# The causal mask of the differential attention: added on VectorE in PSUM, or accumulated by identity products on TensorE

## The chip, the cores and the metric

The kernel runs on one core of one Trainium2 chip. The metric is the time of one execution on the device in microseconds, as the median of several runs.

## What is computed

A decoder trunk of two layers over 512 tokens of width 1024, in fp32. Layer 0 mixes tokens with an mLSTM, layer 1 with a causal differential softmax attention; both also attend to 256 memory tokens, and both end with a gated feed-forward block. The part of the change is the differential attention, cut here to what matters:

```python
def diff_attention(h, positions, w_in, q_norm, k_norm, lam_vecs, subln, lambda_init):
    p = h @ w_in
    q = rope(rmsnorm(p[..., :768].reshape(B, S, 12, 64), q_norm), positions)
    k = rope(rmsnorm(p[..., 768:1536].reshape(B, S, 12, 64), k_norm), positions)
    v = p[..., 1536:2304].reshape(B, S, 6, 128)
    def block(qblk, bi):                                   # 128 query rows
        s = einsum('bhqd,bhkd->bhqk', qblk, kh) * scale
        s = where(key_idx[None, :] <= q_idx[:, None], s, -inf)      # the causal mask
        pr = softmax(s, axis=-1).reshape(B, 6, 2, 128, S)
        a = pr[:, :, 0] - lam * pr[:, :, 1]
        return einsum('bhqk,bhke->bhqe', a, vh)
```

## The kernel before

The program is written by hand for each engine: one instruction stream per engine, and semaphores between them. The order of the work is the order of the statements in each stream; no planner moves it.

*Dense tiles.* Every projection is a row of tiles of 128 output columns. A tile (`h_tile`, `a_tile`, through `tile`, lines 1265 to 1282) runs over eight blocks k of 128 input rows, and for each it issues three products with a moving side of 512 columns (high weight by high input, high by low, low by high), so 24 in all. All of them, and every other plain product, go through the helper `mm` and show as line 1248. GpSimd splits each weight tile into w_hi and w_lo (lines 461 and 464); it starts a split when TensorE has finished the tile two before (`dense_done`). VectorE takes a finished tile out of PSUM and scales it (`scaled_out`, line 907).

*The differential attention.* It runs over six heads, c = 0 to 5, each of two half heads of 64 rows. Its steps are threaded between the products of the next head's three dense tiles q, k and v: `in_q`, `in_k` and `in_v` are called after the three products of block k of a tile. Per head, TensorE issues four score blocks `b_s(c, u)`, u = 0 to 3, which belong to the query rows t = 3 - u and have (t + 1) x 128 columns: 512, 384, 256 and 128. Block u writes the banks b and b + 1 with b = 6 - 2 (u % 2), so blocks 0 and 2 share banks 6 and 7, and blocks 1 and 3 share 4 and 5. In the k tile stand block 0 (after k = 4) and block 1 (after k = 7, the tile's end), in the v tile block 2 (after k = 0) and block 3 (after k = 2). Blocks 2 and 3 wait until ScalarE has finished the exponentials of the block two before (`bexp`, line 1590). The last head has no dense tile behind it: blocks 2 and 3, the transposes and two small sums stand in a row (lines 1655 to 1664).

For each block, VectorE (`b_max`, lines 1177 to 1185) waits for `bs_done`, adds the mask to the diagonal 128 columns in PSUM (line 1182), takes the maximum of each row (line 1184) and scales it (line 1185, a product of 128x2 elements). `link` is a helper that makes VectorE wait for its own last instruction. ScalarE takes the exponentials (`b_exp`, line 745), VectorE forms the difference of the two probabilities (`b_prob`, lines 1194 to 1196), TensorE transposes it (`b_t`, line 1604), ScalarE copies it out as ATB (line 754), and `b_pv` (line 1611, shown as line 1248) multiplies it with the values, VB. `b_ss` sums the squares of q and k with a selector of 2 columns, half_sel (shown as line 1248, from QS). VectorE's order in a head is block 0's maximum, the k tile taken out, then `b_max` 1, `b_prob` 0, `b_max` 2, `b_prob` 1, `b_max` 3, `b_prob` 2 and 3 (lines 1218 to 1226).

`ident` and `neg_mask` are 128x128 fp32 constants in SBUF, parts of the tile `cn`: the identity, and -1e30 above the diagonal with 0 elsewhere.

Of the kernel before, what the change touches and what calls it, by code (L numbers as in the profile page):

```python
# [28 lines left out]
ALU = mybir.AluOpType  # L29
# [3 lines left out]
P = 128  # L33
# [87 lines left out]
def hybrid_trunk(nc, x, mem, positions, w_out, w_mem_kv, w_gate_up, w_down, a_w_in, a_gate_b, b_w_in,  # L121
                 b_lambda, prm_rows, con, out):
    ctx = ExitStack()
    with ctx:
        def sb(name, shape, dt=F32, scope=ctx):
            return scope.enter_context(nc.sbuf_tensor(name, shape, dt))
# [4 lines left out]
        PS = ctx.enter_context(nc.psum_tensor("PS", [P, 8, 512], F32))  # L131
# [24 lines left out]
        ident = cn[:, C_ID:C_ID + P]  # L156
# [3 lines left out]
        neg_mask = cn[:, C_NEG:C_NEG + P]  # L160
# [43 lines left out]
        QR = sb("QR", [P, 2, SEQ], scope=sB)  # L204
# [616 lines left out]
        def _(dve):  # L821
            link_n = [0]

            def link(ins):
                link_n[0] += 1
                ins.then_inc(vch, 1)
                dve.wait_ge(vch, link_n[0])
# [349 lines left out]
            def b_max(c, u):  # L1177
                t, b = NT - 1 - u, 6 - 2 * (u % 2)
                n = 4 * c + u
                dve.wait_ge(bs_done, n + 1)  # L1180
                dg = PS[:, b:b + 2, t * P:(t + 1) * P]
                link(nc.vector.tensor_tensor(dg, dg, neg_mask.rearrange("p (a n) -> p a n", a=1).broadcast_to([P, 2, P]), ALU.add))
                j = (8 * c + 2 * u) % 64
                link(nc.vector.tensor_reduce(nmB[:, j:j + 2], PS[:, b:b + 2, 0:(t + 1) * P], AX.X, ALU.max, negate=True))  # L1184
                nc.vector.tensor_tensor(nmB[:, j:j + 2], nmB[:, j:j + 2], rqk_all[:, 0, t], ALU.mult).then_inc(bmax, 1)  # L1185
# [19 lines left out]
            for c in range(MC):  # L1205
                n = T_B + 3 * (c + 1)
                last = c + 1 == MC
                if c == 0:
                    dve.wait_ge(trig, 2)
                b_rope(c)  # L1210
                b_norm(c)
                if c >= 1:
                    b_onorm(c - 1)
                scaled_out(n, xqB[:, 0] if last else QKP[:, (c + 1) % 2, 0])
                b_knorm(c)
                if c >= 1:
                    b_lo(c - 1)
                b_max(c, 0)
                scaled_out(n + 1, xqB[:, 1] if last else QKP[:, (c + 1) % 2, 1])
                b_max(c, 1)  # L1220
                b_prob(c, 0)
                b_max(c, 2)
                b_prob(c, 1)
                b_max(c, 3)
                b_prob(c, 2)
                b_prob(c, 3)
                if not last:
                    if c >= 1:
                        dve.wait_ge(bvt_done, c)
                    scaled_out(n + 2, t512[2 + (c + 1) % 2])  # L1230
# [15 lines left out]
        def _(pe):  # L1246
            def mm(out_, a, b, start=True, stop=True):
                return nc.tensor.matmul(out_, a, b, start=start, stop=stop)  # L1248
# [50 lines left out]
            for k in range(KD):  # L1299
                pe.wait_ge(msq_done, k // 2 + 1)  # L1300
                last = mm(PS[:, 3, 0:MEM], ones[:], msq[:, k], start=k == 0, stop=k == KD - 1)
# [52 lines left out]
            for i, row in enumerate((tmp[6], tmp[0])):  # L1354
                for t in range(NT):
                    last = nc.tensor.transpose(PS[:, 3, (i * NT + t) * MH:(i * NT + t + 1) * MH], row[0:MH, t * P:(t + 1) * P],
                                               ident[0:MH, 0:MH])
# [225 lines left out]
            def b_s(c, u):  # L1583
                t, b = NT - 1 - u, 6 - 2 * (u % 2)
                if u == 0:
                    pe.wait_ge(bkr, c + 1)
                if u == 1 and c >= 1:
                    pe.wait_ge(bmix_lo, c)
                if u >= 2:
                    pe.wait_ge(bexp, 2 * (4 * c + u - 2) + 2)  # L1590
                for hd in range(2):
                    r = 64 * hd
                    last = mm(PS[:, b + hd, 0:(t + 1) * P], QR[r:r + 64, 0, t * P:(t + 1) * P], QR[r:r + 64, 1, 0:(t + 1) * P])
                last.then_inc(bs_done, 1)

            def b_t(c, u):
# [17 lines left out]
            for c in range(MC):  # L1614
                n = T_B + 3 * (c + 1)
# [11 lines left out]
                def in_k(k):  # L1627

                    if k < 2:
                        b_kbc(c, 2 * k)  # L1630
                        b_kbc(c, 2 * k + 1)
                    if c >= 1 and k in (2, 3):
                        b_oturn(c - 1, 2 * (k - 2))
                        b_oturn(c - 1, 2 * (k - 2) + 1)
                    if k == 4:
                        b_s(c, 0)
                    if k in (5, 6):
                        b_vt(c, 2 * (k - 5))
                        b_vt(c, 2 * (k - 5) + 1)
                    if k == 7:  # L1640
                        b_s(c, 1)

                def in_v(k):

                    if k in (0, 2):
                        b_s(c, 2 + k // 2)
                    if k in (5, 6):
                        b_t(c, k - 5)
# [72 lines left out]
```

## Time and profile before

| | us |
|---|---|
| median of 3 runs | 1361.65 |
| lowest and highest run | 1358.72, 1362.04 |
| span of the profiled execution | 1360.3 |
| TensorE busy (products) | 1288.3 |
| TensorE busy (weight loads) | 1029.4 |
| VectorE busy | 654.4 |
| GpSimd busy | 724.3 |
| ScalarE busy | 344.8 |

A timeline row gives start and duration in us, with equal neighbours merged ("x4"), and in brackets the idle time before it and what ended it. A group row ends with the idle time before its instructions and who ended that. Lines are those of the kernel before.

### The profile page before, as it was taken

To read this page: it belongs to the slowest core of one execution; us is meant where nothing else is said; L and a number is where in the kernel's file an instruction comes from. 1 tells how busy PE (TensorE), PEld (TensorE's weight loads), DVE (VectorE), ACT (ScalarE), POOL (GpSimd) and SP (SyncE) were. 2 spreads that over 40 slices of the span, in tenths; PEclk is the share of its full clock that TensorE was granted. 3 is DMA by queue.
4 is the path that set the end of the run, shared out by engine and by line. 5 is a ranking of instruction groups with operands and counts; after the bars stand their busy time and mean duration, and the time that the engine had idled before them with its cause. 6 is when DMAs were issued, how large, how long until landed. Compare 5 with 4: busy or idle time off the path is not lost.

```text
span 1360.3 us, 16185 instructions
## 1 busy us (share of the span) xinstructions
PE 1288.3 (95%) x5865; PEld 1029.4 (76%) x5865; DVE 654.4 (48%) x804; ACT 344.8 (25%) x679; POOL 724.3 (53%) x422
## 2 busy tenths in 40 slices
PE   5789999988999999999999799988999999999998
PEld 5667767666888888888887577666888888888886
DVE  6788812365734213322368777773753313331331
ACT  5332312355222001100122444456232100100101
POOL 5555543223666666666666333430666666666663
PEclk9898989998999999999999899998999999999999
DMA  8322221111333333333233222220333333333322
GB/s 246 83 62 77 79 77 31 47 47 31 94 97 103 93 93 94 106 94 93 87 106 111 65 73 78 64 76 0 93 93 94 93 96 105 93 93 95 102 74 86
DMA packets 217840, 116.34 MB, mean 86 GB/s; under 512 B 3912, under 2 KB 216002, under 8 KB 217794
## 3 DMA queue, kind: packets, MB, share of 16 engines
q1 hardware_dynamic: 216208, 111.69, 28.4%
q10 hardware_dynamic: 1586, 4.07, 1.1%
q8 instruction: 26, 0.43, 0.1%
q14 instruction: 20, 0.16, 0.0%
HBM read 110.50 MB, written 2.10 MB: 83 GB/s over the span
## 4 chain that ended last, share of the span: by engine, by line
PE 78%; DVE 14%; ACT 3%; issue 2%; POOL 1%; DMA 1%; ACTq 0%; DVEq 0%; POOLq 0%
PE PS L1248 76%; DVE QK L927 2%; DVE acc L870 2%; DVE Al L847 1%; DVE QK L924 1%; POOL w_lo L464 1%; DVE nmB L1185 1%; DVE tmp L917 1%; POOL w_hi L461 1%; DVE nmB L1184 1%; DMA prm<-in_rows_dram 1%; DVE kvs L898 0%; DVE xT L1083 0%; PE PS L1604 0%; DVE Al L1021 0%
## 5 line engine op out<-in xcount | busy, mean ns | idle before, releaser
L461 POOL TENSOR_SCALAR w_hi<-w_raw 128x1024 fp32r<-128x1024 f32 (+1 forms) x207 | 218.7, 1057 | 606.2 <-PE PS L1248 597.5
L464 POOL TENSOR_TENSOR w_lo<-w_raw,w_hi 128x1024 fp32r<-128x1024 f32 (+1 forms) x207 | 505.3, 2441 | 17.3
L1248 PE MATMUL PS<-Hh,w_hi 128*128 128x512 f32 x1080 | 437.5, 405 | 17.2 <-issue 8.1
L1248 PE MATMUL PS<-Hh,w_lo 128*128 128x512 f32 x1080 | 423.6, 392 | 0.0
L1248 PE MATMUL PS<-Hl,w_hi 128*128 128x512 f32 x1080 | 423.5, 392 | 0.0
L1248 PEld LDWEIGHTS PS<-Hh,w_hi 128*128 128x128 f32 x1080 | 204.8, 190 | 72.3 <-issue 22.1
L1248 PEld LDWEIGHTS PS<-Hh,w_lo 128*128 128x128 f32 x1080 | 204.3, 189 | 43.9
L1248 PEld LDWEIGHTS PS<-Hl,w_hi 128*128 128x128 f32 x1080 | 205.0, 190 | 38.3 <-issue 0.7
L1248 PE MATMUL PS<-Ah,w_hi 128*128 128x512 f32 (+1 forms) x544 | 209.8, 386 | 8.8 <-DVE kv L856 4.4
L1248 PE MATMUL PS<-Ah,w_lo 128*128 128x512 f32 (+1 forms) x544 | 205.9, 379 | 0.0
L1248 PE MATMUL PS<-Al,w_hi 128*128 128x512 f32 (+1 forms) x544 | 205.9, 378 | 0.0
L1248 PEld LDWEIGHTS PS<-Ah,w_hi 128*128 128x128 f32 x544 | 103.3, 190 | 33.9 <-issue 4.6
L1099 DVE TENSOR_TENSOR tmp<-PS,rinv 128x512 f32<-128x512 f32 x44 | 30.4, 692 | 200.4 <-PE PS L1248 200.4
L1248 PEld LDWEIGHTS PS<-Ah,w_lo 128*128 128x128 f32 x544 | 103.3, 190 | 19.0
L1248 PEld LDWEIGHTS PS<-Al,w_hi 128*128 128x128 f32 x544 | 103.4, 190 | 17.5
L691 ACT ACTIVATE tmp<-tmp 128x512 f32<-128x512 f32 x44 | 27.9, 634 | 317.7 <-DVE tmp L1097 317.7
L1105 DVE TENSOR_TENSOR Al<-tmp,Ah 128x512 f32 x44 | 82.3, 1871 | 40.1 <-ACT Ah L693 40.1
L693 ACT ACTIVATE Ah<-tmp 128x512 f32 x44 | 27.9, 633 | 251.6 <-DVE tmp L1102 251.6
L1114 DVE TENSOR_TENSOR xT<-xT,PS 128x512 f32 x32 | 22.0, 688 | 137.9 <-PE PS L1248 137.9
L870 DVE TENSOR_TENSOR acc<-acc,tmp 128x512 f32<-128x512 f32 x28 | 67.5, 2411 | 14.7 <-ACT tmp L518 14.7
L1097 DVE TENSOR_TENSOR tmp<-PS,rinv 128x512 f32<-128x512 f32 x44 | 30.4, 692 | 53.8 <-PE PS L1248 53.4
L518 ACT ACTIVATE tmp<-xT 128x512 f32<-128x512 f32 x32 | 20.3, 635 | 101.9 <-DVE xT L1083 91.8
(249 smaller groups left out, 1077.3 us busy)
## 6 DMA issues: line engine op xcount, KB each, us to landing
w_raw<-in_w_gate_up_dram SPq DMA_DIRECT2D x88, 512.0 KB, 3.8
w_raw<-in_w_down_dram SPq DMA_DIRECT2D x32, 512.0 KB, 3.6
w_raw<-in_a_w_in_dram SPq DMA_DIRECT2D x27, 512.0 KB, 3.8
w_raw<-in_b_w_in_dram SPq DMA_DIRECT2D x20, 512.0 KB, 3.8
w_raw<-in_w_out_dram SPq DMA_DIRECT2D x16, 512.0 KB, 3.6
w_raw<-in_w_down_dram SPq DMA_DIRECT2D x16, 384.0 KB, 3.1
w_raw<-in_w_mem_kv_dram SPq DMA_DIRECT2D x8, 512.0 KB, 7.9
QKR<-QKP ACTq DMA_DIRECT2D x24, 128.0 KB, 4.8
```

Of the source, the lines that this page charges most:

```text
L461: nc.gpsimd.tensor_scalar(w_hi[:, sl, 0:nk], w_raw[:, raw, 0:nk], 0.0, 1.0, ALU.add, ALU.mult).then_inc(w_round, 1)
L464: nc.gpsimd.tensor_tensor(w_lo[:, sl, 0:nk], w_raw[:, raw, 0:nk], w_hi[:, sl, 0:nk].bitcast(F32), ALU.subtract).then_inc(w_split, 1)
L518: nc.scalar.activation(tmp[6 + n % 2][:, 0:SEQ], xT[:, k], ACT.Square).then_inc(xsq, 1)
L691: nc.scalar.activation(tmp[0][:, 0:SEQ], tmp[1][:, 0:SEQ], ACT.Silu).then_inc(silu_done, 1)
L693: nc.scalar.activation(Ah[:, bass.ds(i, 1)], tmp[3][:, 0:SEQ].rearrange("p (a n) -> p a n", a=1), ACT.Copy).then_inc(f_hi, 1)
L870: nc.vector.tensor_tensor(acc[:], acc[:], sq, ALU.add).then_inc(xsq_used, 1)
L927: nc.vector.scalar_tensor_tensor(y, raw[:, tap:tap + SEQ], w(R_CW + tap * QKC), y, ALU.mult, ALU.add).then_inc(conv_step if tap else conv_ ...
L1097: nc.vector.tensor_tensor(tmp[1][:, 0:SEQ], PS[:, base % 2], rinv[:], ALU.mult).then_inc(dense_free, 1)
L1099: nc.vector.tensor_tensor(tmp[2][:, 0:SEQ], PS[:, (base + 1) % 2], rinv[:], ALU.mult).then_inc(dense_free, 1)
L1105: nc.vector.tensor_tensor(Al[:, bass.ds(i, 1)], one, Ah[:, bass.ds(i, 1)].bitcast(F32), ALU.subtract).then_inc(f_ready, 1)
L1114: nc.vector.tensor_tensor(xk_, xk_, PS[:, b:b + 1], ALU.add).then_inc(dense_free, 1)
L1248: return nc.tensor.matmul(out_, a, b, start=start, stop=stop)
```

## The change

VectorE no longer adds the mask. In its place TensorE, behind the two score products of a block, issues two more products, one for each half head, with the identity as stationary and the mask as moving side, which accumulate onto the diagonal 128 columns of the scores in PSUM. `bs_done` is raised by the last of these.

```diff
@@ b_max, VectorE @@
                 dve.wait_ge(bs_done, n + 1)
-                dg = PS[:, b:b + 2, t * P:(t + 1) * P]
-                link(nc.vector.tensor_tensor(dg, dg, neg_mask.rearrange("p (a n) -> p a n", a=1).broadcast_to([P, 2, P]), ALU.add))
                 j = (8 * c + 2 * u) % 64
@@ b_s, TensorE @@
                 for hd in range(2):
                     r = 64 * hd
-                    last = mm(PS[:, b + hd, 0:(t + 1) * P], QR[r:r + 64, 0, t * P:(t + 1) * P], QR[r:r + 64, 1, 0:(t + 1) * P])
+                    mm(PS[:, b + hd, 0:(t + 1) * P], QR[r:r + 64, 0, t * P:(t + 1) * P], QR[r:r + 64, 1, 0:(t + 1) * P],
+                       stop=False)
+                for hd in range(2):
+                    last = mm(PS[:, b + hd, t * P:(t + 1) * P], ident, neg_mask, start=False)
                 last.then_inc(bs_done, 1)
```

## Rows read from the trace of the kernel before

**Rows 1.** The page: TensorE's busy time and share, and the ended-last chain by engine.
```profile
PE 1288.3 (95%) x5865; PEld 1029.4 (76%) x5865; DVE 654.4 (48%) x804; ACT 344.8 (25%) x679; POOL 724.3 (53%) x422
...
PE 78%; DVE 14%; ACT 3%; issue 2%; POOL 1%; DMA 1%; ACTq 0%; DVEq 0%; POOLq 0%
```

**Rows 2.** Busy times in a stretch of head 2: length, PE, PEld, DVE, ACT, POOL, clock, DMA.
```profile
815.00:843.00 28.00, 26.75 (x147) 20.32 (x146) 22.12 (x39) 13.18 (x35) 10.18 (x7) 1.00 0.27 76
```

**Rows 3.** TensorE's waits, 759 to 918 us: waiting line, releaser, us in total, times, longest.
```profile
PE PS L1248 <- ACT PB L745: 8.8, 6, 2.6
```

**Rows 4.** Timeline, TensorE, head 2: start us, us, engine, line, op, tiles, shape, count [idle].
```profile
822.54 0.92 PE L1248 MATMUL PS<-QR 64*128 64x384 f32 x4
823.38 0.50 PE L1248 MATMUL PS<-Hh,w_hi 128*128 128x512 f32 x1
...
824.28 0.70 PE L1248 MATMUL PS<-QR 64*128 64x256 f32 x4
...
825.94 0.39 PE L1248 MATMUL PS<-Hl,w_hi 128*128 128x512 f32 x1
826.17 0.40 PE L1248 MATMUL PS<-Hh,w_lo 128*128 128x512 f32 x1
827.82 0.49 PE L1248 MATMUL PS<-QR 64*128 64x128 f32 x4 [1.25 <-ACT PB L745]
828.25 0.50 PE L1248 MATMUL PS<-Hh,w_hi 128*128 128x512 f32 x1
```

**Rows 5.** Timeline, TensorE, head 2: fp32 products of 128 rows, narrow and wide.
```profile
835.90 0.50 PE L1248 MATMUL PS<-cn,QS 128*128 128x2 f32 x4
836.26 0.48 PE L1248 MATMUL PS<-Hh,w_hi 128*128 128x512 f32 x1
...
837.41 2.48 PE L1248 MATMUL PS<-VB,ATB 128*128 128x128 f32 x20
839.64 0.47 PE L1248 MATMUL PS<-Hh,w_hi 128*128 128x512 f32 x1
```

**Rows 6.** Groups by line and form, 759 to 918 us: the mask addition (count | busy us, mean ns).
```profile
L1182 DVE TENSOR_TENSOR PS<-PS,cn 128x256 f32<-128x256 f32 x24 | 10.3, 429 | 5.9 <-PE PS L1248 5.9
```

**Rows 7.** Timeline, VectorE, head 2, around the second score block.
```profile
823.50 0.43 DVE L1182 TENSOR_TENSOR PS<-PS,cn 128x256 f32<-128x256 f32 x1 [0.16 <-PE PS L1248]
823.97 0.96 DVE L1184 TENSOR_REDUCE nmB<-PS 128x2 f32<-128x768 f32 x1
824.96 1.36 DVE L1185 TENSOR_TENSOR nmB<-nmB,rqk_all 128x2 f32<-128x2 f32 x1
```

**Rows 8.** Line L1185 of VectorE: shortest, median and longest of its 24 instructions, in ns.
```profile
L1185 DVE TENSOR_TENSOR nmB<-nmB,rqk_all x24: 160/161/1360, 765.4 to 915.5; 128x2 f32<-128x2 f32 x24
```

**Rows 9.** Timeline, GpSimd, heads 1 and 2: the weight split that runs beside block 1.
```profile
795.77 2.38 POOL L464 TENSOR_TENSOR w_lo<-w_raw,w_hi 128x1024 fp32r<-128x1024 f32 x1
...
822.77 1.06 POOL L461 TENSOR_SCALAR w_hi<-w_raw 128x1024 fp32r<-128x1024 f32 x1 [4.60 <-PE PS L1248]
823.91 2.39 POOL L464 TENSOR_TENSOR w_lo<-w_raw,w_hi 128x1024 fp32r<-128x1024 f32 x1
```

**Rows 10.** Timeline, TensorE, last head, from its fourth score block on.
```profile
912.17 0.80 PE L1248 MATMUL PS<-QR 64*128 64x128 f32 x4 [2.62 <-ACT PB L745]
...
914.67 0.90 PE L1604 MATMUL PS<-cn,PB 128*128 128x128 f32 x3 [0.66 <-DVE PB L1196]
...
917.27 0.88 PE L1604 MATMUL PS<-cn,PB 128*128 128x128 f32 x3 [0.20 <-ACT ATB L754]
918.57 4.13 PE L1248 MATMUL PS<-VB,ATB 128*128 128x128 f32 x20 [0.43 <-ACT ATB L754]
922.63 1.99 PE L1248 MATMUL PS<-xk,xqB 64*128 64x256 f32 x8
```

**Rows 11.** Stretches of 1 us in the last head: clock in the column before the DMA share.
```profile
910.00:911.00 1.00, 0.00 (x0) 0.00 (x0) 0.96 (x3) 0.30 (x1) 0.65 (x1) 1.00 0.00 0
...
912.00:913.00 1.00, 0.83 (x5) 0.61 (x6) 0.96 (x3) 0.63 (x3) 0.00 (x0) 0.50 0.85 254
```

## The prediction

> **What bounds the kernel now.** I read the page first. TensorE is busy for 1288.3 us and holds 78% of the chain that ended last; VectorE holds 14% [rows 1]. That is an average over stages, so I went to the stage of the change, the differential attention from 759 to 918 us: six heads (c = 0 to 5), each with four score blocks (u = 0 to 3, of 512, 384, 256 and 128 columns). In the stretch of head 2, TensorE is busy for 26.75 of 28 us at the full clock, and VectorE for 22.12 [rows 2]. One head takes 28.1 us: the same step of GpSimd starts at 795.77 and 823.91 [rows 9]. The list of TensorE's waits says where the rest is: six waits on the exponentials of line 745, 8.8 us together, which is one per head, 1.25 us in a steady head and 2.6 in the last [rows 3, 4, 10]. So in heads 0 to 4 TensorE sets the pace with one stall per head, and work that is added to TensorE costs its full time unless it falls into that stall. VectorE's saving counts only through the stall.
>
> Where the stall lies decides the sum. The timeline of TensorE shows the order: block 1 starts at 822.54, block 2 at 824.28, the last weight product before the stall at 826.17, then nothing until block 3 at 827.82 [rows 4]. Weight products follow each other every 0.23 us (825.94, 826.17). Behind block 1 the three products from 823.38 to block 2 take 0.90 us and not 0.69: 0.11 is a weight load that isn't hidden behind a score block, 0.10 the change to the next one. So block 3 could have started at 826.17 + 0.23 + 0.10 = 826.50, and the spare time is 1.32 us. Block 3 waits for the exponentials of block 1, since both use banks 4 and 5. These follow line 1185 of block 1, which ends at 824.96 + 1.36 = 826.32 [rows 7]. Line 1185 is a product of 128x2 elements. Its median is 161 ns and here it takes 1360 [rows 8]. GpSimd's subtraction of a weight tile runs from 823.91 to 826.30 [rows 9], and line 1185 ends 0.02 us after it; both read two SBUF tensors. The end of the stall is therefore pinned by GpSimd, whose split was released by the end of the k tile, ahead of block 1, and not by VectorE's own length.
>
> **The change part by part.** *Removed:* 24 additions on VectorE, 429 ns each, 10.3 us in all [rows 6], and one link wait each: from the addition's start to that of the reduction are 0.47 us [rows 7]. *Added:* two fp32 products per block on TensorE, 48 in all, stationary the identity of 128x128, moving the 128x128 mask. The semaphore bs_done moves to the last of them. No DMA, buffer or instruction of ScalarE or GpSimd is added or moved.
>
> The price of a mask product. The nearest row is the product of weights and values: same type, same 128x128 stationary, same 128 columns. Ten of them leave 20 records, and the next product starts 2.23 us later (837.41 to 839.64) [rows 5], or 0.112 us a record and 0.223 a product. Two fp32 products with only 2 moving columns take 0.36 us until the next product starts [rows 5], nearly the 0.45 of a pair with 128 columns. The price hangs on the weight load, not on the columns. A block of two mask products costs 0.446 us. The load of 0.11 us that is exposed behind a score block today is exposed once after the change too, so it cancels. From below the bound is the column time: from a score block to the next product are 0.43 us with 128 columns (827.82 to 828.25) and 0.84 with 384 (822.54 to 823.38) [rows 4], so 128 columns more cost four records 0.205 us, and the four of a mask block would cost 0.21. A block could cost less than that only by running beside other products, and TensorE's records follow each other in order, which excludes a gain here. From above: 0.89, if each product took twice the records seen. I take 0.446, of the row with the same shape.
>
> *Block 0 (heads 0 to 5).* TensorE goes on with the k tile after it and waits for nothing. The two products are exposed: +0.446 us. On VectorE the result comes 0.446 later and the addition's 0.47 is gone, so its maximum is ready at the same moment; ScalarE and all behind it stay.
>
> *Blocks 1 and 2 (heads 0 to 4).* Both are issued between the k tile and the stall. Block 1's scores come 0.446 later, the reduction starts at 823.94 in place of 823.97, and line 1185 is held until 826.30 as before. The stall ends at the same distance from the k tile; 0.89 us of mask work comes ahead of it and takes 0.89 of the 1.32 us of spare time. Cost: 0, and the cover is not used up (0.43 left). Were it gone, up to 0.89 a head would come on top. Queued behind TensorE's wait for block 3 is the rest of the v tile, the same as now.
>
> *Block 3 (heads 0 to 4).* It starts when the stall ends and nothing waits behind it: +0.446 us. VectorE saves two additions after the stall, 0.9 us, so the transposes of the weights, which TensorE reaches 0.45 later, find them ready. What is late next is nothing that I can see; TensorE is the bound until the next head's stall. The dense tiles that follow shift with it.
>
> *Head 5.* It has no v tile, and TensorE waits four times: 2.62, 0.66, 0.20 and 0.43 us [rows 10]. Block 0 costs 0.446. Blocks 1 and 2 vanish in the 2.62. Block 3 runs at the half clock [rows 11]. There 20 records take 4.06 us (918.57 to 922.63) [rows 10], so it costs 0.81, against 0.66 of wait behind it. That wait is for VectorE, which is one addition ahead there, and two ahead at the waits of 0.20 and 0.43. I take back 0.3 more than block 3 costs (bounds 0 and 0.7). Head 5: +0.45 - 0.3 = +0.15.
>
> *The sum.* 5 heads x 2 exposed blocks x 0.446 = 4.46, and 0.15: +4.6 us. The profiled execution has a span of 1360.3 us, which becomes 1364.9. The runs' median is 1361.65, 1.35 above that span, so 1366.2 us on the runs. That is 0.34% more, and 0.3% (4.1 us, 1365.7) is about what a measurement of this kernel can tell from no change. The runs of before themselves lie 3.3 us apart.
>
> The Trainium skill would price a record lower: its page "TensorE: Matmul & The Clock Gate" (Back-to-back issue gap) gives about 81 ns for a pair of weight load and product with 128 columns. By it a block would be 0.32 us, and the ten exposed ones 3.2 us. The trace has 112 ns for this shape and type, and the sum goes by the trace.
>
> **The rivals.**
>
> *The clock stays up in the last head (not slower).* TensorE falls to half its clock, from 2.4 to 1.2 GHz, between 911 and 913 us after standing still [rows 11]. With the masks of blocks 1 and 2 the engine stands still for 1.7 us and not 2.6. If the clock then holds, the weights-and-values product takes 2.23 us in place of 4.06, and the waits ahead of it shrink by some 0.8 to 1.2. That is -2.6 us on head 5: 4.6 - 2.6 = +2.0, or 1363.7 us. It decides if the clock's fall is later than 919 us in the new trace. Against it: several waits remain between short products in 912 to 918. 0.14.
>
> *A mask product costs only its columns.* Same stationary twice, small moving tile: 0.21 a block gives 10 x 0.21 + 0.1 = 2.2, or 1363.9 us. Against it: products with 2 columns cost nearly as much as those with 128 [rows 5]. 0.08.
>
> *The stall does not cover.* If line 1185 is not pinned by GpSimd but follows from when its inputs are ready and then always takes 1.36 us, the end of the stall still stays (+0.446 - 0.47). Only if the hold starts anew behind the mask does it move: the stall then ends 0.45 to 0.9 later, all four blocks count, 20 x 0.446 = 8.9 and 0.5 for head 5, or 1371 us. Against it: 826.30 and 826.32 agree to 0.02 us [rows 7, 9]. 0.10.
>
> *An fp32 product takes four passes.* Then a block costs 0.89, two are 1.78 in a spare time of 1.32, and a head pays 2 x 0.89 + 0.46 = 2.24; five heads 11.2 and about 1 in the last: 1374 us. In the trace the same product has two records of 0.112 us each, so I give it 0.03. The Trainium skill states this rule: "FP8 and Floating Point Precision" (TensorE Precision Notes) has true fp32 at four passes through the array. By that rule the sum would be the one of this rival; the trace disagrees with it.
>
> *Faster.* By over 0.3% would need 8.7 us below the forecast. The half clock would have to go in both later dips, and I find no row that promises it. 0.03.
>
> **How the numbers follow.** Forecast 0.62, clock 0.14, columns only 0.08, no cover 0.10, four passes 0.03, faster 0.03 (sum 1.00). The forecast's own spread is about 1 us around 1366.2, with the border at 1365.7, so two thirds of it (0.42) is slower and 0.20 the same. Slower: 0.42 + 0.10 + 0.03 = 0.55. Same: 0.20 + 0.14 + 0.08 = 0.42. Faster: 0.03. The range takes in the clock case with its spread below and the case without cover above: 1362 to 1371 us. What is outside is the four passes, the faster case and some tails.
>
> **What the new profile would show.** Right: after each score block in heads 0 to 4, four more records of TensorE, 128x128 by 128 columns, with 0.44 to 0.45 us until the next product; the period of a head at 29.0 us; TensorE's wait before block 3 at about 0.4 us; line 1185 of block 1 (now two lines higher) still ending with GpSimd's subtraction; VectorE's busy time in the stage lower by 10.3 us. Wrong: a period near 28.5 (cheap products), near 29.9 (no cover) or above 30 (four passes); a clock in the last head that does not fall (first rival). If the period is 29.0 and the time still differs by more than 2 us, the difference lies in the dips of the clock behind 910 us.

## The result and the profile after

| | before | after |
|---|---|---|
| median of 17 runs, us | 1360.73 | 1364.46 |
| lowest and highest run, us | 1356.55, 1363.22 | 1361.56, 1367.37 |
| span of the profiled execution, us | 1360.3 | 1364.3 |

The ratio of the runs is 1.0031, with a 95% interval from 1.0020 to 1.0042: slower by 0.31%, or 4.2 us, where 4.6 was forecast (the two medians alone differ by 3.7). The profiled spans differ by 4.0 us.

The page of the changed kernel, its busy times:

```profile
PE 1297.1 (95%) x5961; PEld 1038.3 (76%) x5961; DVE 643.3 (47%) x780; ACT 344.8 (25%) x679; POOL 725.7 (53%) x422
```

TensorE is busy 8.8 us longer and VectorE 11.1 us shorter than in [rows 1], and the time follows neither. A stretch of 28 us in head 2 (length; busy time and count of PE, PEld, DVE, ACT and POOL; clock, DMA share, GB/s), and the waits of TensorE from 759 to 923 us (waiting line, releaser, us in total, times, longest):

```profile
820.00:848.00 28.00, 27.68 (x158) 21.39 (x157) 20.14 (x34) 13.17 (x35) 9.56 (x7) 1.00 0.27 76
```

```profile
PE PS L1246 <- ACT PB L745: 3.2, 6, 1.6
```

TensorE is busy 27.68 us of 28, where [rows 2] have 26.75. Its six waits on the exponentials shrink from 8.8 us [rows 3] to 3.2. The timeline of TensorE in head 2 shows where the added products went (start us, us, engine, line, op, tiles, shape, count, idle before):

```profile
825.19 0.92 PE L1246 MATMUL PS<-QR 64*128 64x384 f32 x4
826.04 0.71 PE L1246 MATMUL PS<-cn 128*128 128x128 f32 x4
826.50 0.48 PE L1246 MATMUL PS<-Hh,w_hi 128*128 128x512 f32 x1
...
827.38 0.70 PE L1246 MATMUL PS<-QR 64*128 64x256 f32 x4
828.01 0.71 PE L1246 MATMUL PS<-cn 128*128 128x128 f32 x4
...
830.43 0.49 PE L1246 MATMUL PS<-QR 64*128 64x128 f32 x4 [0.32 <-ACT PB L745]
830.86 0.71 PE L1246 MATMUL PS<-cn 128*128 128x128 f32 x4
831.32 0.48 PE L1246 MATMUL PS<-Hh,w_hi 128*128 128x512 f32 x1
```

Each mask block is four records named `PS<-cn`. Two numbers carry the case. Block 1's mask starts at 826.04 and the next weight product at 826.50, so a block takes 0.46 to 0.47 us here. The net is slightly less: from block 1 to block 2 are 2.19 us (825.19 to 827.38), where they were 1.74 [rows 4], so the mask adds 0.45, and the head period below gives 0.44. And the wait before block 3 is 0.32 us, where it was 1.25 [rows 4]. VectorE's reduction and the small product of block 1, and GpSimd's subtraction beside them:

```profile
826.79 0.96 DVE L1182 TENSOR_REDUCE nmB<-PS 128x2 f32<-128x768 f32 x1 [0.80 <-PE PS L1246]
827.78 1.15 DVE L1183 TENSOR_TENSOR nmB<-nmB,rqk_all 128x2 f32<-128x2 f32 x1
```

```profile
826.55 2.36 POOL L464 TENSOR_TENSOR w_lo<-w_raw,w_hi 128x1024 fp32r<-128x1024 f32 x1
```

The small product (now line 1183) ends at 828.93, GpSimd's subtraction at 828.91: the same 0.02 us as in [rows 7, 9]. VectorE now idles 0.80 us before the reduction, where it idled 0.16 before the addition. Of the 0.64 us more, 0.47 are the addition that it no longer does. The other 0.17 are new: the reduction starts 1.60 us after block 1's first product (825.19), and the addition started 0.96 after it (822.54, 823.50), so the mask makes the scores 0.64 us late and not only the 0.45 that it costs TensorE. GpSimd's hold covers this too.

### The profile page after: what moved, and what is told of

Same layout as the page of the kernel before. It is cut to its first block, busy times and chain, and to the rows that moved or that the text cites. A ratio compares the mean times of both kernels' runs of the same rounds, so it can differ in the third digit from the quotient of the medians.

```text
span 1364.3 us, 16353 instructions
## 1 busy us (share of the span) xinstructions
PE 1297.1 (95%) x5961; PEld 1038.3 (76%) x5961; DVE 643.3 (47%) x780; ACT 344.8 (25%) x679; POOL 725.7 (53%) x422
## 4 chain that ended last, share of the span: by engine, by line
PE 78%; DVE 13%; ACT 3%; issue 2%; POOL 1%; DMA 1%; ACTq 0%; DVEq 0%; POOLq 0%
PE PS L1246 76%; DVE QK L927 2%; DVE acc L870 2%; DVE Al L847 1%; DVE QK L924 1%; POOL w_lo L464 1%; DVE tmp L917 1%; DVE nmB L1183 1%; POOL w_hi L461 1%; DMA prm<-in_rows_dram 1%; PE PS L1605 1%; DVE kvs L898 0%; DVE nmB L1182 0%; DVE xT L1083 0%; DVE Al L1021 0%
```

## Where the 4.0 us of the profiled pair are

The first two rows below are of the kernel before: block 0 of head 0, and block 0 of the last head; the third is the first product of the output projection behind the attention.

```profile
762.51 1.13 PE L1248 MATMUL PS<-QR 64*128 64x512 f32 x4
...
903.16 1.13 PE L1248 MATMUL PS<-QR 64*128 64x512 f32 x4
...
946.10 0.50 PE L1248 MATMUL PS<-Ah,w_hi 128*128 128x512 f32 x1
```

The kernel after: block 0 of head 0, then from block 0 of the last head to the same product of the output projection:

```profile
762.94 1.13 PE L1246 MATMUL PS<-QR 64*128 64x512 f32 x4
...
907.96 1.13 PE L1246 MATMUL PS<-QR 64*128 64x512 f32 x4
...
917.41 0.49 PE L1246 MATMUL PS<-QR 64*128 64x128 f32 x4 [1.60 <-ACT PB L745]
...
919.45 0.90 PE L1605 MATMUL PS<-cn,PB 128*128 128x128 f32 x3 [0.47 <-DVE PB L1194]
...
921.71 0.88 PE L1605 MATMUL PS<-cn,PB 128*128 128x128 f32 x3
923.02 3.86 PE L1246 MATMUL PS<-VB,ATB 128*128 128x128 f32 x20 [0.43 <-ACT ATB L754]
926.81 1.99 PE L1246 MATMUL PS<-xk,xqB 64*128 64x256 f32 x8
...
950.17 0.50 PE L1246 MATMUL PS<-Ah,w_hi 128*128 128x512 f32 x1
```

Block 0 of head 0 starts 0.43 us later than before: that lies ahead of everything the change touches. From there to the last head's block 0 are 145.02 us and not 140.65: +4.37 for five heads, 0.87 each (forecast 0.89). From that block to the output projection are 42.21 us and not 42.94: -0.73 (forecast +0.15). The rest of the program gives 0.07 back. 0.43 + 4.37 - 0.73 - 0.07 = 4.0.

The 0.73 us can be followed through the rows. Up to the second batch of transposes nothing changes: it starts 11.51 us after block 0 before (914.67 and 903.16) and 11.49 after (919.45 and 907.96). In both kernels TensorE waits for VectorE there, and the one addition of 0.47 us that VectorE has saved by then pays for block 0's mask. From there to the third batch are 2.26 us and not 2.60: the wait for ScalarE's copy (0.20 us [rows 10]) is gone, because VectorE is a second addition ahead and the copy starts 0.48 us earlier in the head (12.89 us after block 0, 13.37 before). The product of weights and values takes 3.79 us (923.02 to 926.81) in place of 4.06 [rows 10], and all that follows up to the output projection 0.11 less.

The clock moved as well. Two stretches of 1 us of the kernel after (the clock is the column after the five engines):

```profile
918.00:919.00 1.00, 0.98 (x8) 0.75 (x8) 0.93 (x4) 0.82 (x3) 0.00 (x0) 1.00 1.07 322
919.00:920.00 1.00, 0.55 (x3) 0.55 (x4) 0.96 (x4) 0.42 (x3) 0.00 (x0) 0.54 0.02 4
```

TensorE falls from 2.4 to 1.2 GHz at about 919 us; before, it was at 0.50 from 912 on [rows 11]. With the shift of 4.8 us taken off, that is some 2.5 us later, so block 3 of the last head, its mask and the first transposes run at the full clock. But a late fall is not the only way to such a gain. In the run with blocks 0 and 3 on TensorE (below), the clock had fallen ahead of block 3 (granted 0.50 from 916 to 917 us), and the last head, from block 0 to the output projection, still takes 42.30 us:

```profile
907.55 1.13 PE L1249 MATMUL PS<-QR 64*128 64x512 f32 x4
...
917.00 0.80 PE L1249 MATMUL PS<-QR 64*128 64x128 f32 x4 [2.62 <-ACT PB L745]
917.73 1.22 PE L1249 MATMUL PS<-cn 128*128 128x128 f32 x4
...
949.85 0.50 PE L1249 MATMUL PS<-Ah,w_hi 128*128 128x512 f32 x1
```

Block 3's mask takes 1.02 us there until the next product, at half the clock, and the waits of 0.66 and 0.20 us behind it are gone. Up to the product of weights and values (923.12) the last head takes 15.57 us in that run, 15.41 before and 15.06 after. The rest of its gain lies in that product, 3.52 us, during which the clock rises. So of the 0.73 us up to 0.5 can be the late fall, and no run separates it from VectorE's lead. One profile of each does not tell how much repeats: the product of weights and values of the last head takes between 3.5 and 4.6 us over the profiles of this case.

## The experiments

In all of them the head period is the distance between block 0 of one head and of the next. It repeats to 0.05 us within a profile unless said otherwise, and it is the sharpest measure here; the ratios have an interval of 0.1 to 0.2% to each side. It is 28.13 us before and 29.00 after.

**Only blocks 1 and 2 on TensorE.**

```diff
 b_max:
+                if u in (0, 3):
                     dg = PS[:, b:b + 2, t * P:(t + 1) * P]
                     link(nc.vector.tensor_tensor(dg, dg, neg_mask..., ALU.add))
 b_s:
+                if u in (1, 2):
+                    for hd in range(2):
+                        last = mm(PS[:, b + hd, t * P:(t + 1) * P], ident, neg_mask, start=False)
```

> Kernel before, but the masks of score blocks 1 and 2 go to TensorE; blocks 0 and 3 keep VectorE's addition. Theory (the stall ahead of block 3 covers blocks 1 and 2): the head period stays at 28.13 us as in the kernel before, TensorE's wait before block 3 is 0.3 to 0.4 us, the last head gains 0 to 0.5 us, and the time is that of before within 0.1% (ratio 0.999 to 1.001). Rival (every mask block costs TensorE its 0.44 us wherever it stands, the wait only moves): period 29.0 us, ratio about 1.003. Rival (cost shared evenly over four blocks): period 28.57 us, ratio 1.0015.

Ratio 1.0006 (0.9996 to 1.0017), period 28.11 us. Blocks 0, 3 and the next 0 in TensorE's timeline:

```profile
786.26 1.13 PE L1249 MATMUL PS<-QR 64*128 64x512 f32 x4
...
795.29 0.49 PE L1249 MATMUL PS<-QR 64*128 64x128 f32 x4 [0.32 <-ACT PB L745]
...
814.36 1.13 PE L1249 MATMUL PS<-QR 64*128 64x512 f32 x4
```

The two blocks are in the program, the period is that of before, and the wait before block 3 fell from 1.25 to 0.32 us. Mask work in the stall costs nothing. The last head gained 0.66 us (42.28 against 42.94), a little more than the 0 to 0.5 expected.

**Only blocks 0 and 3 on TensorE.** The same edit with the blocks exchanged.

> Kernel before, but the masks of score blocks 0 and 3 go to TensorE; blocks 1 and 2 keep VectorE's addition. Theory (only blocks 0 and 3 are exposed): head period 29.0 us, that of the changed kernel, with TensorE's wait before block 3 at 1.25 us as before; about +4.4 us over the five heads, ratio 1.003 to 1.004. Rival (shared evenly): period 28.57, ratio 1.0015.

Ratio 1.0023 (1.0012 to 1.0034), period 29.02 us:

```profile
791.48 1.13 PE L1249 MATMUL PS<-QR 64*128 64x512 f32 x4
...
800.98 0.49 PE L1249 MATMUL PS<-QR 64*128 64x128 f32 x4 [1.23 <-ACT PB L745]
...
820.51 1.13 PE L1249 MATMUL PS<-QR 64*128 64x512 f32 x4
```

The full loss per head with half of the added products, and the wait is still 1.23 us. The ratio is below the 1.003 to 1.004 expected, though its interval reaches into that; the 0.64 us that the last head gains (42.30 against 42.94) are part of the reason. So the loss of the change is that of blocks 0 and 3. The even split of the cost is out.

**No mask at all.** Both lines of the addition in `b_max` are deleted from the kernel before, and nothing is put in their place.

> The causal mask is left out altogether, on both engines (this part of the computation is missing). Theory (the end of the stall is pinned by GpSimd's subtraction): head period 28.13 us as before, though VectorE is 0.47 us shorter per block; the product of 128x2 elements in block 1 then takes about 1.8 us and still ends with GpSimd's subtraction; only the last head gains, 0.3 to 0.9 us; ratio 0.9993 to 1.0. Rival (VectorE's own length sets the end of the stall): the stall shrinks by 0.47 us, period 27.66 us, -2.4 us and the last head on top, ratio 0.998.

Ratio 0.9992 (0.9982 to 1.0002), period 28.13 us. VectorE's reduction and small product of block 1, and GpSimd's subtraction:

```profile
794.70 0.96 DVE L1182 TENSOR_REDUCE nmB<-PS 128x2 f32<-128x768 f32 x1 [0.16 <-PE PS L1246]
795.69 1.81 DVE L1183 TENSOR_TENSOR nmB<-nmB,rqk_all 128x2 f32<-128x2 f32 x1
```

```profile
795.10 2.38 POOL L464 TENSOR_TENSOR w_lo<-w_raw,w_hi 128x1024 fp32r<-128x1024 f32 x1
```

Without the addition VectorE starts both steps 0.46 us earlier in the head, the small product takes 1.81 us in place of 1.36, and it still ends with GpSimd's subtraction (797.50 and 797.48). VectorE's 10.3 us of additions in [rows 6] cost the kernel before nothing in heads 0 to 4. In these heads there was nothing for the change to win. The last head gained 0.71 us (42.23 against 42.94).

**The small product in another form, in all blocks.** In the kernel before, line 1185 becomes two instructions that read one SBUF tensor and a scalar of one column each:

```diff
-                nc.vector.tensor_tensor(nmB[:, j:j + 2], nmB[:, j:j + 2], rqk_all[:, 0, t], ALU.mult).then_inc(bmax, 1)
+                for hd in range(2):
+                    ins = nc.vector.tensor_scalar(nmB[:, j + hd:j + hd + 1], nmB[:, j + hd:j + hd + 1],
+                                                  rqk_all[:, 0, t, hd:hd + 1], None, ALU.mult)
+                ins.then_inc(bmax, 1)
```

> Kernel before with VectorE's addition kept in all blocks; only the product of 128x2 elements that reads two SBUF tensors is written as two tensor_scalar instructions of 128x1, each with one SBUF tensor and one scalar of a column. Theory (that product is held because it reads two SBUF tensors while GpSimd's subtraction runs): in block 1 it takes 0.2 to 0.35 us in place of 1.36, the stall ahead of block 3 shrinks by about 1.0 us to 0.2, the head period falls to 27.1 to 27.3 us unless a later wait appears before the last transposes, and the time falls by 4 to 5 us (ratio 0.9965 to 0.997). Rival (the 1.36 us have another cause, such as the write or the position behind the reduction): period 28.1 to 28.5 us, ratio 1.000 to 1.001.

Ratio 1.0147 (1.0125 to 1.0169): slower by 20 us (18 between the medians), where 4 to 5 us faster was expected. TensorE's waits, then VectorE (block 1's split product, and the last two steps of the same head), then GpSimd:

```profile
PE PS L1607 <- DVE PB L1199: 6.9, 5, 1.4
PE PS L1251 <- ACT PB L745: 1.2, 5, 0.2
```

```profile
831.42 0.33 DVE L1186 TENSOR_SCALAR nmB<-nmB,rqk_all 128x1 f32<-128x1 f32 x2
...
838.92 0.76 DVE L1198 TENSOR_SCALAR PB<-PB,rsB,lam 128x128 f32<-128x128 f32 x1
839.71 2.48 DVE L1199 SCALAR_TENSOR_TENSOR PB<-PB,rsB 128x128 f32<-128x128 f32 x1
```

```profile
838.33 1.27 POOL L461 TENSOR_SCALAR w_hi<-w_raw 128x1024 fp32r<-128x1024 f32 x1 [5.59 <-PE PS L1251]
839.68 2.36 POOL L464 TENSOR_TENSOR w_lo<-w_raw,w_hi 128x1024 fp32r<-128x1024 f32 x1
```

Half of the expectation came true. The split product takes 0.33 us in place of 1.36 while GpSimd subtracts (830.36 to 832.74), and the waits before block 3 in heads 0 to 4 fell from 1.23 to 1.25 us each to 0.23. This agrees with the rule of the Trainium skill's page "SBUF — State Buffer" (Who interferes with whom): a VectorE instruction with two SBUF inputs contends with a GpSimd instruction that reads SBUF, one with at most one such input, outside the 2-port modes, does not. The form with one SBUF tensor is not free of the hold by itself, though: VectorE's next step, a tensor_scalar of 128x512, takes 1.16 us in this run (from 831.86, over the end of GpSimd's subtraction) and 0.55 in the changed kernel (829.04), where the subtraction has ended. No trace shows in which mode it runs.

What I had not worked out is the end of the head. TensorE arrives about 1 us earlier at the end of the v tile, so GpSimd begins its next split earlier too, but VectorE has hardly become faster: line 1198 starts 13.70 us after block 0 (838.92), and 13.77 before. Its last two steps (lines 1198 and 1199 of this kernel) now meet it: the first runs until 839.68, when w_hi is done, and the second starts at 839.71, just behind GpSimd's subtraction of 839.68, and takes 2.48 us for 128x128 elements. TensorE waits up to 1.4 us for it before the last transpose, then its clock falls in four of the five heads (granted 0.90 to 0.94 over a head, 1.00 over head 0), and the period goes to 29.4, 32.6, 30.9, 31.0 and 32.6 us.

**The same in block 1 alone.**

```diff
+                if u == 1:
+                    (the two tensor_scalar as above)
+                else:
                     nc.vector.tensor_tensor(nmB[:, j:j + 2], nmB[:, j:j + 2], rqk_all[:, 0, t], ALU.mult).then_inc(bmax, 1)
```

> Kernel before with all four additions on VectorE; only block 1's product of 128x2 elements is split. Theory (the split gains at the stall and loses at the end of the head, because VectorE with its four additions begins its last combination behind GpSimd's next subtraction): TensorE waits about 0.2 us before block 3 and over 1 us for line 1196 before the last transpose, the clock falls in some heads, head period above 29 us, ratio 1.005 to 1.015. Rival (the late hold in the run with all products split came from the 0.17 us that each further split costs): no late wait, period 27.0 to 27.1 us, ratio about 0.996.

Ratio 1.0079 (1.0058 to 1.0100), periods 29.14, 32.38, 29.13, 32.35 and 29.17 us. GpSimd, then VectorE's last two steps of head 1:

```profile
804.87 1.04 POOL L461 TENSOR_SCALAR w_hi<-w_raw 128x1024 fp32r<-128x1024 f32 x1 [5.60 <-PE PS L1254]
```

```profile
805.10 0.89 DVE L1201 TENSOR_SCALAR PB<-PB,rsB,lam 128x128 f32<-128x128 f32 x1
806.03 2.48 DVE L1202 SCALAR_TENSOR_TENSOR PB<-PB,rsB 128x128 f32<-128x128 f32 x1
```

The last combination takes 2.47 to 2.48 us in heads 0 to 4, and TensorE waits for it once in each, 7.5 us in all. The extra instructions of the other blocks were not the cause of the hold; with them the loss is larger (1.47% against 0.79%), and why is not shown.

**Block 1 split, and block 2's mask on TensorE.** The edit above, and from the change only u == 2 (blocks 0, 1 and 3 keep VectorE's addition).

> Kernel before, but in block 1 alone the product of 128x2 elements is two tensor_scalar instructions, and the mask of block 2 alone goes to TensorE. Theory (the split product frees the stall of 1.3 us; the run with all products split lost it again because VectorE's last combination of a head started behind GpSimd's next subtraction and was held by it for 2.5 us, and 0.5 us less work on VectorE avoids that): TensorE has no wait before block 3 or one below 0.1 us, VectorE's last line 1196 of a head takes at most 1.3 us, and the head period is 28.13 - 1.32 + 0.45 = 27.3 us, 4 us over the five heads less than before (ratio 0.9965 to 0.9975). Rival (the split product always provokes the late hold): a wait of TensorE on VectorE before the last transpose of 1 us or more, period 29 us or more, ratio above 1.004.

Ratio 0.9964 (0.9948 to 0.9981): 4.9 us faster than before. The period is 27.28 us, and TensorE has no idle time in head 2 (stretch of 28 us, columns as above). The second row is VectorE's last combination of a head:

```profile
815.00:843.00 28.00, 28.00 (x156) 21.41 (x155) 21.71 (x39) 13.16 (x35) 10.99 (x7) 1.00 0.28 76
```

```profile
802.98 1.21 DVE L1203 SCALAR_TENSOR_TENSOR PB<-PB,rsB 128x128 f32<-128x128 f32 x1
```

It starts 0.03 us before GpSimd's first step of the split (803.01), is held by that, and ends before the subtraction: 1.21 us and not 2.48. Against the run with block 1 alone split, VectorE's last two steps come 0.49 us earlier in the head, nearly all of it the addition, and GpSimd's split 0.15 us later, since TensorE has a mask block more. So the step before the combination is done (802.94) before the split starts, where in that run it began 0.23 us behind the split's start and was held. These 0.6 us decide between 27.28 and over 29 us; no run separates the two parts.

**The changed kernel with block 1 split.** All masks on TensorE.

> Changed kernel (all masks on TensorE), with the product of 128x2 elements split in block 1. Theory: the last 0.3 to 0.4 us of stall before block 3 go, TensorE runs through the head without a wait, period 28.6 to 28.65 us; that is 2 us less than the changed kernel and 2.4 us more than before (ratio to before 1.001 to 1.002). It shows the four mask blocks at full price: 28.13 - 1.32 + 4 x 0.446 = 28.6. Rival (late hold as in the run with all products split): period above 29.5 us.

Ratio 1.0005 (0.9989 to 1.0020), period 28.62 us, and TensorE has no wait in heads 0 to 4. This is the sum of the prediction with all four blocks at full price: 28.13 - 1.32 + 4 x 0.446 = 28.59. By it the ratio should be 1.001 to 1.002; it came out below that, with both values in its interval.

**Narrow mask products.** In the changed kernel, 2 moving columns, so that most of the mask is missing from the result: `mm(PS[:, b + hd, t * P:t * P + 2], ident, neg_mask[:, 0:2], start=False)`.

> Changed kernel, but each mask product has 2 moving columns in place of 128, so most of the mask is left out of the computation. Theory (the price is that of the four weight loads): the records of a block still take 0.42 to 0.47 us until the next product, head period 28.9 to 29.0 us. Rival (price by columns): 0.1 us or less a block, period 28.2 to 28.3 us. If the price is 0.36 as for the products of line 1554 in the kernel before, the period is 28.8 to 28.9.

Ratio 1.0038 (1.0023 to 1.0053), period 29.01 us. A mask block and the weight product behind it:

```profile
793.07 0.61 PE L1246 MATMUL PS<-cn 128*128 128x2 f32 x4
793.54 0.48 PE L1246 MATMUL PS<-Hh,w_hi 128*128 128x512 f32 x1
```

0.47 us, the same as with 128 columns. The four weight loads of the block begin at 793.07 and the next load at 793.51, 0.11 us apart; with 128 columns they do the same (826.04, 826.48). So a block costs four records, and 64 times fewer columns change nothing. The price by columns is out. That the weight load is what fills the 0.11 us, and not another fixed time of a record, is argued: no run changes the size of the load. The Trainium skill's page "TensorE: Matmul & The Clock Gate" (LDWEIGHTS) has a weight load at its columns divided by 1.2 GHz, by which an estimate for 128 columns is 107 ns; the 0.11 us a record agree with that, and not with the 81 ns of the same page that the prediction set beside them.

**Mask products of type fp32r.** In the changed kernel, ScalarE makes rounded copies `idr` and `mkr` of the identity and the mask once, and the products take these.

> Changed kernel, but identity and mask are rounded copies of type fp32r, made once by ScalarE ahead of the attention. Theory (the price is 0.112 us a record, and an fp32r product leaves one record where an fp32 one leaves two): a block costs 0.22 us, blocks 1 and 2 lie in the stall (wait before block 3 about 0.8 us), head period 28.13 + 2 x 0.22 = 28.57 us, 2.2 us less than the changed kernel, ratio to before about 1.0015. Rival (same price per product whatever the type): period 29.0 us.

Ratio 1.0022 (1.0006 to 1.0037), period 28.57 us, wait before block 3 at 0.78 us:

```profile
789.08 0.44 PE L1252 MATMUL PS<-mkr,idr 128*128 128x128 f32 x2
789.36 0.46 PE L1252 MATMUL PS<-Hh,w_hi 128*128 128x512 f32 x1
```

Two records in place of four, and 0.43 us less per head, from the two exposed blocks. The price is per record: 0.11 us.

**The best of it together.** Block 1 split, only block 2's mask on TensorE, and that in fp32r.

> Kernel before with block 1's product of 128x2 elements split and only block 2's mask on TensorE, there with identity and mask as rounded copies of type fp32r made once by ScalarE. Theory: one mask block at 0.22 us in place of 0.45, head period 27.28 - 0.22 = 27.06 us; ratio to before 0.995 to 0.9965. Rival (TensorE meets the exponentials of block 1 again, or the late hold comes back since TensorE is 0.22 us earlier): period 27.3 us or more, with a wait before block 3 or before the last transpose.

Ratio 0.9953 (0.9939 to 0.9966), median 1354.98 us against 1361.33: 6.4 us faster than the kernel before. Period 27.10 to 27.15 us (27.06 was expected); block 3 has no wait before it:

```profile
797.68 0.49 PE L1261 MATMUL PS<-QR 64*128 64x128 f32 x4
```

TensorE runs through heads 0 to 4 without a wait, and the late hold did not come back (VectorE's last combination takes 1.02 to 1.07 us). It beats both kernels; against the run with an fp32 mask in block 2 the two intervals overlap, and the period alone (27.12 against 27.28) says that it is ahead.

## Why the prediction held

*The bound and the stall.* TensorE set the pace and one stall per head was the only cover: right. The period of 29.0 us was named and measured at 29.00, the wait before block 3 at about 0.4 and measured at 0.32.

*The price of a block.* 0.446 us from the product of weights and values; 0.44 measured, and the narrow and the fp32r run show what it goes by: 0.11 us a record, each with a weight load, whatever the columns. The scores came later by more than this price, 0.64 us and not 0.446, so block 1's maximum was 0.17 us late where I had it 0.03 early; nothing waited for it. The four passes are out: two records a product at 0.11 us, where four passes would have given a period above 30. This is where the trace differs from the Trainium skill's page "FP8 and Floating Point Precision" (TensorE Precision Notes), which has true fp32 at four.

*Blocks 1 and 2 hidden, 0 and 3 exposed.* Right, shown from both sides by the runs with either pair. The end of the stall is pinned by GpSimd: without a mask it stays, and with the split product, which GpSimd does not hold, it moves.

*VectorE's saving is worth nothing.* Right in heads 0 to 4. The statement that nothing new waits behind block 3 held for this change, but it rested on VectorE's being ahead there; the split product alone took that lead away, and I had no term for it.

*Head 5.* This term was mis-sized: +0.15 forecast, -0.73 in the profiled pair. Block 3 comes 0.44 us later, as forecast. From block 3 to the output projection I took back 0.3 and 1.17 came back (33.93 us before, 32.76 after): 0.79 of it up to the product of weights and values, where block 3's mask ran at the full clock and the waits for VectorE and ScalarE gave more than I took, and 0.38 in that product and behind it, which vary from profile to profile. The first rival came half true: the clock fell at 919 us, some 2.5 us later than the shifted fall of before, but it also stayed low through most of the product of weights and values, so the 1.8 us that the rival had for that product were 0.27. I had block 3's mask at 0.81 us; it took 0.55 at the full clock here (917.83 to 918.38) and 1.02 at half of it in the run with blocks 0 and 3.

*The total.* That 4.2 us were measured where 4.6 was forecast is in part luck. The stage of the change gave 4.37 - 0.73 = 3.6 us in the profiled pair, and 0.43 us from ahead of it made this 4.0. The result also lies on the border of 0.3% that the prediction drew between slower and the same: 0.31%, with an interval from 0.20 to 0.42.

*From the profiled execution to the runs.* I took 1.35 us between span and run; the profiled run after has 1366.04 us for a span of 1364.3, so it is 1.7. The median of before moved from 1361.65 (3 runs) to 1360.73 (17 runs). The forecast of 1366.2 is thus 1.7 us above the median of 1364.46, of which 0.9 lie in the basis.

## What to carry to other kernels

A small product on TensorE was priced here by its records, 0.11 us each, and not by its columns up to 128; read that price from a product of the same type and stationary shape in the trace. Work added to the bounding engine is free only in front of a wait whose end another engine pins; find that wait, name who pins it, and put the work there and nowhere else. And when a stall is removed, look one step on: the engine that now comes earlier starts others earlier, and an engine that has kept its own pace can fall behind them.

## What the runs showed of the hardware that was not expected

*What VectorE meets on GpSimd is worth up to 2.1 us.* VectorE's combination of 128x128 elements (two SBUF tensors) takes 0.35 us alone, 1.0 to 1.2 when it meets GpSimd's w_hi step, even if it began 0.03 us before it, and 2.48 when it comes 0.03 us behind the start of the subtraction. GpSimd can lose too: its subtraction in the split that the end of the v tile releases takes 2.68 us in the changed kernel, where VectorE's rotary products began 0.58 us before it (836.52 and 837.10), and 2.39 in the kernel before, where they began 0.58 us after it (834.62 and 834.04).

*The clock ahead of the change.* The same unchanged program part has a different granted clock from execution to execution. Before, and below it the run with blocks 1 and 2 on TensorE (clock in the column before the DMA share):

```profile
175.00:200.00 25.00, 23.89 (x91) 15.62 (x90) 4.02 (x6) 4.83 (x12) 11.06 (x7) 0.90 0.31 85
```

```profile
175.00:200.00 25.00, 23.89 (x101) 16.46 (x99) 4.44 (x7) 4.84 (x12) 12.29 (x7) 1.00 0.32 85
```

Block 0 of head 0 starts between 756.5 and 763.3 us over the profiles of this case, though all is the same up to there but for two copies of ScalarE in the fp32r runs. That spread is larger than the effect; the period of a head, which repeats to a few hundredths, is what made the parts of the change readable.
